# One level of Strassen's algorithm in both GEMMs of an MLP on one Trainium2 core

## The reference, cut to what matters

```python
for l in range(DEPTH):                       # DEPTH = 1, SEQ = 2048, D_MODEL = 1024, D_FF = 4096
    h = rmsnorm(x, norm_mix[l])
    proj = jnp.einsum('bsd,de->bse', h, w_in[l])
    ...                                      # two groups of attention heads -> mixed
    x = x + jnp.einsum('bse,ed->bsd', mixed, w_out[l])
    h = rmsnorm(x, norm_mlp[l])
    u = jax.nn.relu(jnp.einsum('bsd,df->bsf', h, w_up[l]))
    x = x + jnp.einsum('bsf,fd->bsd', u * u, w_down[l])
return rmsnorm(x, norm_final)
```

## Time and profile before

| | us |
|---|---|
| median of 3 runs | 2750.29 (2746.88 to 2752.5) |
| span of the profiled execution | 2750.6 |
| PE busy | 2609.6 (95%) |
| DVE busy | 1395.4 (51%) |
| ACT busy | 924.9 (34%) |
| POOL busy | 156.4 (6%) |

### The profile page before, as it was taken

One profiled execution on the slowest core, in us unless ns is written; L12 is line 12 of the kernel. 1 busy time (PEld: TensorE's weight loads), 2 busy tenths in 40 slices (PEclk: granted clock), 3 DMA queues, 4 the chain that ended last, 5 costly groups with the idle time before them and its releaser, 6 DMA issues.

```text
span 2750.6 us, 36080 instructions
## 1 busy us (share of the span) xinstructions
PE 2609.6 (95%) x12624; PEld 2158.9 (78%) x12624; DVE 1395.4 (51%) x2476; ACT 924.9 (34%) x1669; POOL 156.4 (6%) x244
## 2 busy tenths in 40 slices
PE   7999997799999996898999999999999999999997
PEld 6788885688888885777788888888878888888886
DVE  6311111688887885455445444444454454444545
ACT  5211111688888885222221212111131212121211
...
DMA packets 122489, 301.43 MB, mean 110 GB/s; under 512 B 10776, under 2 KB 72984, under 8 KB 108952
## 3 DMA queue, kind: packets, MB, share of 16 engines
...
q0 software_dynamic: 6144, 16.79, 2.6%
...
## 4 chain that ended last, share of the span: by engine, by line
PE 51%; DVE 0%; ACT 0%; DMA 0%; POOL 0%; issue 0%; ACTq 0%; POOLq 0%
PE f_ps_u L1634 26%; PE f_ps_d L1649 25%; DMA out<-f_y 0%; DVE f_y L1582 0%; DVE f_wd_lo L1559 0%; ACT f_wd_hi L1501 0%; ACT f_y L1520 0%; POOL f_rstd L1481 0%; DVE f_wu_lo L1554 0%; ACT f_wu_hi L1495 0%; DVE f_acc L1577 0%; POOL f_rstd L1478 0%; ACTq L1346 0%; POOLq L1474 0%; POOLq L1477 0%
## 5 line engine op out<-in xcount | busy, mean ns | idle before, releaser
L1577 DVE TENSOR_TENSOR f_acc<-f_acc,f_ps_d 128x512 f32<-128x512 f32 x512 | 343.3, 686 | 223.4 <-PE f_ps_d L1649 223.4
L1634 PE MATMUL f_ps_u<-h_hi_kept,f_wu_hi 128*128 128x512 f32 x1024 | 406.3, 397 | 4.0 <-DVE f_wu_lo L1554 4.0
L1649 PE MATMUL f_ps_d<-f_wd_hi,f_u_hi 128*128 128x512 f32 x1024 | 401.1, 392 | 8.8 <-DVE f_wd_lo L1559 8.8
L1634 PE MATMUL f_ps_u<-h_lo_kept,f_wu_hi 128*128 128x512 f32 x1024 | 405.9, 396 | 0.0
L1634 PE MATMUL f_ps_u<-h_hi_kept,f_wu_lo 128*128 128x512 f32 x1024 | 405.9, 396 | 0.0
L1649 PE MATMUL f_ps_d<-f_wd_lo,f_u_hi 128*128 128x512 f32 x1024 | 400.9, 392 | 0.0
L1649 PE MATMUL f_ps_d<-f_wd_hi,f_u_lo 128*128 128x512 f32 x1024 | 400.2, 391 | 0.0
L1509 ACT ACTIVATE f_r<-f_ps_u 128x512 f32<-128x512 f32 x128 | 76.4, 597 | 958.2 <-PE f_ps_u L1634 958.2
L1568 DVE TENSOR_TENSOR f_sq<-f_r 128x512 f32<-128x512 f32 x128 | 88.6, 692 | 395.4 <-ACT f_r L1509 393.9
L874 DVE TENSOR_TENSOR a_pt_lo<-a_ps_t,a_pt_hi 128x512 fp32r<-128x512 f32 (+3 forms) x384 | 234.6, 618 | 95.1 <-ACT a_pt_hi L963 92.6
L352 PE MATMUL p_ps_o<-p_ht_hi,p_w_hi 128*128 128x512 f32 x608 | 238.7, 393 | 3.0 <-DVE p_w_lo L270 3.0
...
## 6 DMA issues: line engine op xcount, KB each, us to landing
wu_raw_kept<-in_w_up SPq DMA_DIRECT2D x32, 1024.0 KB, 7.3
f_wd_raw<-in_w_down SPq DMA_DIRECT2D x32, 1024.0 KB, 5.0
proj_hi<-p_o_hi SPq DMA_DIRECT2D x18, 1024.0 KB, 4.0
proj_lo<-p_o_lo SPq DMA_DIRECT2D x18, 1024.0 KB, 6.7
p_w_raw<-in_w_in SPq DMA_DIRECT2D x19, 512.0 KB, 7.9
p_x_in<-in_x SPq DMA_DIRECT2D x16, 512.0 KB, 4.2
a_k_hi_fox<-proj_hi SPq DMA_DIRECT2D x16, 512.0 KB, 12.0
a_k_lo_fox<-proj_lo SPq DMA_DIRECT2D x16, 512.0 KB, 13.7
```

The costliest lines, as they stand in the source:

```text
L1577: nc.vector.tensor_tensor(acc[:, t, cols], acc[:, t, cols], ps_d[n % RING][:], ALU.add).then_inc(added, 1)
L1634: last = nc.tensor.matmul(ps_u[n][:], w[:, k, f * P:(f + 1) * P], h[:, k, s * BANK:(s + 1) * BANK], start=(k == 0 and m == 0), stop=(k == ...
L1649: last = nc.tensor.matmul(ps_d[n % RING][:], u[parity][:, f, t * P:(t + 1) * P], w[:, f, half * BANK:(half + 1) * BANK], start=(f == 0 and ...
```

## The change

Both GEMMs of the MLP are done as one level of Strassen's algorithm in the form with 7 products of half-size blocks and 15 block additions (Winograd's), in two passes one after the other.

In short: (1) **up pass**: 32 groups (2 blocks of tokens, 16 of `w_up` columns), 7 products each, 12 matmuls of 128x512 per product: 2688 matmuls. GpSimd makes the four combinations of the weights (`mix_w`, 128x512 each), the four combinations of the squared results for the second pass (`mix_u`), and the combinations of the tokens (`mix_tokens`, 128x2048 each). ScalarE and VectorE split each weight operand (`split_op`, 128x512) and, where the tokens change, the token operands (`split_hop`, two of 128x1024). The 7 operands of the down GEMM (`u_ops`) are written to DRAM as plain float32. (2) **down pass**: 7 products in the order D1, D6, D7, D5, D3, D2, D4, each for two blocks of tokens and 16 steps, 12 matmuls a step: 2688 matmuls. The operand of a step comes back from DRAM and is split; the weights of a product (`b_hi`, `b_lo`, 16 tiles of 128x512) are loaded, combined by GpSimd (`mix_b`: 2, 1, 1, 0, 0, 3 operations a tile in the order above from D6 on) and split during the second block of the product ahead, out of a ring of three. Each result is added to up to four places of `acc` (L1835), 112 times in all. (3) `mix_out` hands `h` over unsplit; half of it goes through DRAM (`h_rest`), and its last store stands at the end of the stage. Six of the token combinations are made there. All loops of the two stages are unrolled.

```diff
 # mix_out
-            def split_ht(pair, slot, at):          # ACT: h_hi, DVE: h_lo of every tile
...
+            def store_ht(t):                       # SP
+                sp.wait_ge(ht_done, 2 * t + 2)
+                sp.dma_start(h_rest[:, :, bank, :, col:col + P],
+                             stage[:, t % 2].rearrange("p (j k) s -> p j k s", j=2)).then_inc(ht_stored[t % 2], 16)
...
+            store_ht(ST - 1)
+            for slot in range(2):
+                sp.wait_ge(x_stored[slot], 16 * ST // 2)
+                sp.wait_ge(ht_stored[slot], 16 * KEPT // 2)
-def mlp(nc, x_mid, h_hi, h_lo, wu_raw, h_hi_dram, h_lo_dram, w_up, w_down, norm_final, out):
+def feed(nc, x_mid, h_rest, raw, w_raw, hop0_hi, hop0_lo, u_ops, w_up, w_down, norm_final, out):
+    NP, LEAD, RING, A_RING, B_RING = 7, 3, 5, 8, 3
+    UP = GROUPS * NP                               # 224 products up, 224 steps down
...
+        HOP_ORDER = ((1, 2, 3, 4, 5, 6), (0, 1, 3, 2, 5, 4, 6))
+        SWITCH = (FG - 1) * NP
+        hop_at = {-2: (0, 1), 0: (0, 2), 1: (0, 3), 2: (0, 4), 3: (0, 5), 4: (0, 6)}
+        hop_at |= {SWITCH + 1: (1, 0), SWITCH + 2: (1, 1), SWITCH + 4: (1, 3), SWITCH + 5: (1, 2),
+                   SWITCH + 6: (1, 5), SWITCH + 8: (1, 4), SWITCH + 10: (1, 6)}
+        b_at = {((i - 1) * 2 + 1) * FG + j + 1: (i, j) for i in range(1, NP) for j in range(FG)}
...
+            def load_b(i, j):                      # SP
+                n = (i - 1) * FG + j
+                sp.wait_ge(b_lo_done, max(FG, FG + n - B_RING + 1))
+                for e, cols in PARTS[i]:
+                    sp.dma_start(b_wide[n % B_RING][:, e, cols], wd_v[j, :, e, cols]).then_inc(b_in[n % B_RING], 16)
...
+            for g in range(GROUPS):                # GpSimd, up pass
+                mix_w(g, 4)
+                if g == 0:
+                    mix_tokens(0, 4)
+                if g == FG - 2:
+                    mix_tokens(1, 1)
+                if g + 1 < GROUPS:
+                    mix_w(g + 1, 1)
+                    mix_w(g + 1, 2)
+                if g == FG - 1:
+                    mix_tokens(1, 2)
+                    mix_tokens(1, 3)
+                if g:
+                    mix_u(g - 1)
+                if g == FG - 1:
+                    mix_tokens(1, 4)
+                if g + 1 < GROUPS:
+                    mix_w(g + 1, 3)
+            mix_u(GROUPS - 1)
+            for i in range(1, NP):                 # GpSimd, down pass
+                if MIXES[i]:
+                    for j in range(FG):
+                        mix_b(i, j)
...
+            for n in range(UP + STEPS):            # VectorE; ScalarE is written alike
+                g, i = divmod(n, NP)
+                if n < UP and i >= 4:
+                    add_up(g, i - 4)
+                if n + LEAD < UP + STEPS:
+                    split_op(n + LEAD)
+                if n in hop_at:
+                    split_hop(*hop_at[n])
+                if n in b_first_at:
+                    for j in b_first_at[n]:
+                        split_b_first(j)
+                q = n - UP
+                if q in b_at:
+                    split_b(*b_at[q])
+                if q >= FG and q % FG < 4:
+                    add_down(q // FG - 1, q % FG)
+                if q in norm_at:
+                    norm(norm_at[q])
...
+            def up(n):                             # TensorE
+                pe.wait_ge(op_lo_done, n + 1)
+                if g % FG == 0:
+                    pe.wait_ge(hop_lo_done, hop_count[g // FG, i])
...
+                for k in range(4):
+                    for m, (w, h) in enumerate(((w_hi, hop_hi), (w_hi, hop_lo), (w_lo, hop_hi))):
+                        last = nc.tensor.matmul(bank[:], w[:, k], h[i][:, k], ...)
+            def down(q):
+                pe.wait_ge(op_lo_done, UP + q + 1)
+                if pair == 0:
+                    pe.wait_ge(b_lo_done, i * FG + j + 1)
...
+                for t in range(4):
+                    for m, (a, w) in enumerate(((op_hi, b_hi), (op_hi, b_lo), (op_lo, b_hi))):
+                        last = nc.tensor.matmul(down_banks[b % 2][t][:], a[:, r, cols], w[j], ...)
```

More of the change, by code:

```diff
@@ L1101, in is_first @@
[L1101 to L1108 removed]
+        ht_done = sem("m_ht_done")
+        ht_stored = [sem(f"m_ht_stored{i}") for i in range(2)]
+        t_mixed = sem("m_t_mixed")
+        hop_hi_done = sem("m_hop_hi_done")
+        hop_lo_done = sem("m_hop_lo_done")
@@ new lines, in root @@
+            def root(e):
+                pool.wait_ge(sums_done, e + 1)
+                nc.gpsimd.tensor_scalar(rstd[:, e:e + 1], ssum[:, e:e + 1], 1.0 / D, EPS,
+                                        ALU.mult, ALU.add).then_inc(meaned, 1)
+                pool.wait_ge(meaned, e + 1)
+                nc.gpsimd.tensor_tensor(rstd[:, e:e + 1], rstd[:, e:e + 1], mhalf[:], ALU.pow).then_inc(rooted, 1)
+            pool.wait_ge(mhalf_set, 1)
+            for which in (1, 2, 3):
+                mix_w(0, which)
@@ new lines, in split_hop, with split_b_first @@
+            def split_hop(pair, i):
+                src = hop_part(pair, i)
+                for half in range(2):
+                    k = slice(2 * half, 2 * half + 2)
+                    dve.wait_ge(hop_hi_done, hop_count[pair, i] - 1 + half)
+                    nc.vector.tensor_tensor(hop_lo[i][:, k], src[:, k], hop_hi[i][:, k].bitcast(F32),
+                                            ALU.subtract).then_inc(hop_lo_done, 1)
+            def split_b_first(j):
+                dve.wait_ge(b_hi_done, j + 1)
+                nc.vector.tensor_tensor(b_lo[j], b_first[:, j % 8], b_hi[j].bitcast(F32),
+                                        ALU.subtract).then_inc(b_lo_done, 1)
@@ new lines, in add_down @@
+            def add_down(b, t):
+                i, pair = divmod(b, 2)
+                if t == 0 and i == 0:
+                    dve.wait_ge(y_in[pair], 16 * NT // 2)
+                if t < 3:
+                    dve.wait_ge(downed, 3 * b + t + 1)
+                else:
+                    dve.wait_ge(prod, UP + (b + 1) * FG)
+                for half, cols in TARGETS[i]:
+                    tile = acc[:, pair * 8 + half * 4 + t, (LO, HI)[cols]]
+                    last = nc.vector.tensor_tensor(tile, down_banks[b % 2][t][:], tile, ALU.add)
+                last.then_inc(added, 1)
@@ L1680, in hybrid_block @@
+        w_raw = [sb(f"wu_raw{i}", [P, 8, 2 * P]) for i in range(2)]
+        hop_hi = sb("hop_hi0", [P, 4, BANK], F32R)
+        hop_lo = sb("hop_lo0", [P, 4, BANK], F32R)
+        mix_out(nc, o_main, o_rest, rsum_inv, w_out, x, norm_mlp, w_up, ident, raw, w_raw, hop_hi, hop_lo,
+                x_mid, h_rest)
+        feed(nc, x_mid, h_rest, raw, w_raw, hop_hi, hop_lo, u_ops, w_up, w_down, norm_final, out)
 def hybrid_block(nc, x, norm_mix, w_in, b_forget, sinks, w_out, norm_mlp, w_up, w_down, norm_final,
```

1018 lines of the change are left out of this document (598 added, 420 removed).

## The result

| | before | after |
|---|---|---|
| median of the runs, us | 2749.22 (2746.88 to 2752.5) | 2615.24 (2613.85 to 2616.27) |
| ratio | | 0.9513, 95% interval 0.9501 to 0.9524 |
| span of the profiled execution, us | 2750.6 | 2612.2 |

The change makes the kernel 4.9% faster. The forecast was 2645 with a range of 2590 to 2715, so the range held it and the forecast was 30 us too slow; the forecast's own range, 2615 to 2680, holds it only just.

A forecast was written before the change was run, and what follows sets the result against it. PE's matmuls bound the kernel (PE busy 95%). 1306.6 + 2.7 + 1237.4 + 17.4 + 16 + 3 + 12 + 6 + 29 + 4 + 10.5 = 2644.6, so 2645 us; own range 2615 to 2680, with rivals 2590 to 2715.

The forecast's parts named there:

- start of the MLP: Handing over from `mix_out`: MLP start moves from 1306.6 by +2.7 us, for a store of 512 KB behind the last copy.
- matmuls: Both passes: 5376 matmuls in place of 6144 at the old rates, 0.2333 up and 0.2270 down: 1237.4 us.
- first group: Up pass start: six token operands split while the group runs, on the port shared with GpSimd: +17.4 us, bounds 5 and 25.
- switch of token blocks: Groups 15 and 16: chain through GpSimd's combinations and VectorE's splits ready at 43 where 30.8 is due: +16, between 3 and 30.
- D6: Down pass, making its weights: load, mixes and splits put the sixteenth tile at 59 where 40.8 is due; lead 6.5: +12 us.
- D7 and D5: Down pass, making their weights: the ring takes 10.1 us for three tiles, 3.4 a tile: +3 us each.
- D4: Down pass, making its weights: port 5.3 us a step, sixteenth tile at 76, lead 6.5: +29 us; DMA second.
- Rival 1: Plain subtractions do not collide with GpSimd; smaller losses in first group, switch, D6 and D4: 2608 us, chance 0.15.
- VectorE and GpSimd keep each other out: Operations reading two SBUF tensors exclude each other, so GpSimd's time and VectorE's splits add; additions from PSUM stay outside.
- Rival 2: Up pass starves a little in every group, 2.0 us uncovered each time, +62: 2707 us, chance 0.15.
- Rival 3: A GpSimd operation of 128x512 takes 2.42 us, as long as 128x1024: 2885 us, slower by 135; chance 0.06.
- Rival 4: The engines hide everything and only matmuls are left: 2565 us, chance 0.04.

The follow-up runs named there:

- e3: Changed kernel with the five 128x2048 token combinations on GpSimd in the MLP touching one column in 512, order and waits kept: 2598.68 us.
- e1: Changed kernel without GpSimd's combinations of the down weights; all loads, splits and matmuls stay: 2593.89 us.
- e2: Changed kernel with half of D4's weights not loaded (512 KB in place of 1 MB a step), the three combinations kept: 2617.06 us.
- e4: Changed kernel with VectorE's `b_lo` split of each D4 weight tile 8 columns wide in place of 512: 2616.92 us.
- e6b: Changed kernel with `f_mhalf` 32 columns wide in place of 1, which moves all tiles allocated behind it in SBUF: 2608.31 us, ratio 0.9484.

## Why the prediction was right, and where its sizes were off

| term | forecast | measured |
|---|---|---|
| start of the MLP | 1309.3 | 1304.7 |
| matmuls | 1237.4 | 1227.7 |
| first group | 17.4 | 2.2 + 13.6 |
| switch of token blocks | 16 | 23.5 |
| up to down | 3 | 0.6 |
| D6 | 12 | 10.3 |
| D7 and D5 | 6 | 0 |
| D4 | 29 | 17.9 |
| clock | 4 | 9.0, in the stages above |
| end | 10.5 | 11.6 |
| sum | 2644.6 | 2612.1 |

1304.7, 2.2 to the first matmul, 1227.7, 66.0 starved (the stages above are rounded) and 11.6 are 2612.2. Fewer matmuls bring the gain, and starving bunched at the named places gives part of it back, as forecast; less of it than forecast.

The total does not tell the mechanism. Rival 1 (plain subtractions do not collide) had 2608, 7 us from the measurement, the forecast 2645, 30 us from it. But rival 1 had 5 for the switch, which cost 23.5, and 9 for the first group, which cost 15.8; that its sum came near is luck: what it had too low there, 24.9 us, is nearly made up by what it had too high in the matmuls (9.7), D7 and D5 (6), the start (4.6) and the clock, which it counts beside the stages (4). The forecast's misses go both ways too: the switch was dearer, D4, the matmuls, D7 and D5 were cheaper.

- **"VectorE and GpSimd keep each other out" was right in kind.** Splits are blocked as the norm was the earlier trace rows, the addition from PSUM is not. e3 shows it by taking the long operations away: the median of the half-operand splits goes from 2290 to 1216 ns. This makes rival 1 false. The Trainium skill (SBUF — State Buffer, Who interferes with whom) says that a VectorE instruction with two SBUF inputs contends with a GpSimd one that reads SBUF; the trace agrees, 5.03 us at most against 0.694 for the addition. The forecast's sign, a maximum near 2 us, was too low: a split can wait for a whole GpSimd operation of 5 us.
- **D4, the largest miss: "Per step the port has 2 x 0.69 and the mixes ... 5.3".** It is 4.62 (e1: GpSimd; e2: not DMA; e4: the price of a split is 0.33 to 0.51 to GpSimd). Adding the full durations of both engines over-counts, since part of a split falls into the gaps of GpSimd's own operations. That is about half of the 11.1 us. VectorE's splits of the fourth and sixteenth tile of D4 end 15.7 and 70.9 us behind the block's first matmul, where the forecast had 13 and 76: the fourth is later, the sixteenth 5.1 earlier. The other half is the lead of PE: the sixteenth is 30.1 us behind the 40.8 where it was due, and PE lost 17.9, so 12.2 were covered and not "6.5". The program shows why: that split stands in VectorE's step 16 of the block, and the next operand split behind it is that of PE's step 20.
- **Switch, 16 for 23.5.** The step that failed is "between them VectorE's 4 splits and 6 half operands, 10.1": I counted undisturbed splits. The 22 half operands of the first group and the switch had a mean of 2201 ns in place of 1220, because GpSimd's operations run beside them. GpSimd's operations on that path were stretched as well, by its timeline: three `mix_tokens` 15.5, one `mix_u` 8.3 and one `mix_w` 1.8 us, where the forecast had 13.8, 5.2 and 1.3. And PE lost 4.3 us at the lower clock there (0.59 in the window of 1630). e3 gives the shares: 12.6 by the token combinations, 10.9 by the rest. My rival had 5 for the case without collisions, and e3 kept some, so neither was tested pure.
- **First group, 17.4 for 15.8.** Half clock makes 3.0 of the measured figure, so the port's sum was too large by more than the total shows, 17.4 for 12.8. e3 took one GpSimd operation of 5 us away there, and 4.3 went.
- **Matmuls, 1237.4 for 1227.7.** "I keep the rates of before by kind" failed in the up pass: 0.2267 for products 0 to 3, 0.2342 for 4 to 6. e6b shows that the second is the tiles' position in SBUF. A rate other than before's was one of the forecast's own signs of being wrong.
- **D7 and D5, 6 for 0.** "The ring takes 10.1 for three tiles" had the collision in full and a load of 5 us in series; the ring kept up with 2.72 a step. No run took this apart; it is read from the spacing.
- **D6, 12 for 10.3.** The chain is the one named (split, load, two combinations, split): 9.0 to 12.8 us for three tiles, with loads of 4.1 to 7.1. That the size is right is in part luck. The fourth tile is split 16.5 us into the block and not at 11, since the 16 additions to `acc`, "the lead covers it", stand in VectorE's order ahead of it; then a tile takes 3.7 and not 4.0, and the lead covers more than 6.5. e1 takes 5.6 away; the 4.7 that stay end in an addition to `acc` that waited for its load.
- **Start, 4.6 early.** 3.5 of it is no work of the change: `mix_out`, whose predecessors are the same code, already began at 1087.8 in place of 1091.3. The rows of 60 to 430 us, before and then after, show it in `project`:

```profile
60.00:430.00 370.00, 367.03 (x1615) 303.52 (x1614) 83.74 (x97) 65.28 (x92) 0.46 (x1) 0.99 0.33 118
```

```profile
60.00:430.00 370.00, 367.03 (x1628) 303.83 (x1627) 84.25 (x97) 65.16 (x92) 0.52 (x1) 1.00 0.33 118
```

  13 matmuls more in the same time, at a granted clock of 1.00 against 0.99. About 1.1 us is left to handing over, which cost 1.6 and not 2.7.
- **Clock, 4 for 9.0.** "After each starved stretch PE may begin at 1.2 GHz": it did at the first product and once more in the first group, twice at the switch (0.59) and once in D6, behind the first of two waits of 2.4 us. In D4 the clock stayed at 1.00 in the window above, though PE waited ten times, up to 1.6 us at a time.
- **End, 10.5 for 11.6.** The small GpSimd operation at L1623 took 633 ns in place of 190; it stands in the chain of the last tile beside VectorE's norm.
- **The other rivals.** Rival 2 is false: between groups 1 and 14 PE waits for nothing, though GpSimd was busy for 161 of 260 us there. Rival 3 is false: an undisturbed GpSimd operation of 128x512 takes 1.28 to 1.29 us, where I took 1.3. Rival 4 is false: 66 us are starved.
